# Gate/up pairs with three 2x2 blocks, and a hidden turn by way of DRAM

## The reference

```
def _swiglu(x, w_gate, w_up, w_down):
    return (jax.nn.silu(x @ w_gate) * (x @ w_up)) @ w_down
x = _layer_norm(DEEPNORM_ALPHA * x + _swiglu(x, w_gate, w_up, w_down), ln2_g, ln2_b)
# x (256, 2048), w_gate and w_up (2048, 5632), w_down (5632, 2048)
```

## Time and profile before

| | |
|---|---|
| median of three runs | 931.42 us (930.88 to 931.42) |
| the profiled execution, its own time | 931.67 us |
| its span, first to last instruction | 929.9 us |
| TensorE busy | 923.4 us, 99% |
| VectorE busy | 773.7 us, 83% |
| ScalarE busy | 513.4 us, 55% |
| GpSimd busy | 95.9 us, 10% |
| moved by DMA | 188.06 MB, mean 202 GB/s |

### The profile page before, as it was taken

One profiled execution on the slowest core, in us unless ns is written; L12 is line 12 of the kernel. 1 busy time (PEld: TensorE's weight loads), 2 busy tenths in 40 slices (PEclk: granted clock), 3 DMA queues, 4 the chain that ended last, 5 costly groups with the idle time before them and its releaser, 6 DMA issues.

```text
span 929.9 us, 11643 instructions
## 1 busy us (share of the span) xinstructions
PE 923.4 (99%) x4406; PEld 774.5 (83%) x4406; DVE 773.7 (83%) x1049; ACT 513.4 (55%) x704; POOL 95.9 (10%) x84
## 2 busy tenths in 40 slices
PE   9999999999999999999999999999999999999997
PEld 8999988888878888888888888888888888888885
DVE  6778566578779898989999998988969997999777
ACT  5686765354464646555565646455545565456550
POOL 0205530000311020202011020000000000000000
PEclk9999999999999999999999999999999999999999
DMA  9744324584808375665648375756657656355632
GB/s 362 315 166 145 129 91 167 195 328 167 318 5 290 111 256 162 223 218 185 228 135 274 112 270 148 242 198 200 219 210 300 226 225 233 130 222 231 230 132 91
DMA packets 36759, 188.06 MB, mean 202 GB/s; under 512 B 4064, under 2 KB 4576, under 8 KB 22880
## 3 DMA queue, kind: packets, MB, share of 16 engines
q1 hardware_dynamic: 36672, 187.32, 56.4%
q0 software_dynamic: 32, 0.00, 0.0%
HBM read 183.11 MB, written 4.19 MB: 201 GB/s over the span
## 4 chain that ended last, share of the span: by engine, by line
PE 99%; DVE 0%; ACT 0%; DVEq 0%; issue 0%; ACTq 0%
PE acc L1983 26%; PE acc L2005 21%; PE acc L1758 9%; PE tp L1983 9%; PE acc L1966 6%; PE acc L1696 5%; PE tp L1966 4%; PE tp L2005 4%; PE acc L1617 4%; PE acc L1895 2%; PE tp L1935 2%; PE acc L1730 1%; PE tp L1809 1%; PE tp L1744 1%; PE tp L1822 1%; PE tp L1606 0%
## 5 line engine op out<-in xcount | busy, mean ns | idle before, releaser
L1983 PE MATMUL acc<-w_hi,act_t 128*128 128x512 f32 x720 | 227.3, 389 | 0.0
L972 ACT ACTIVATE w_hi<-raw 128x1024 fp32r<-128x1024 f32 x120 | 125.7, 1057 | 111.4 <-PE acc L1983 57.2
L1021 ACT ACTIVATE w_hi<-raw 128x512 fp32r<-128x512 f32 (+1 forms) x154 | 114.9, 782 | 100.3 <-PE acc L2005 88.0
L2005 PE MATMUL acc<-w_hi,hid_t 128*128 128x512 f32 x504 | 161.0, 389 | 0.0
L1424 DVE TENSOR_TENSOR w_lo<-raw,w_hi 128x512 fp32r<-128x512 f32 (+1 forms) x154 | 131.8, 881 | 33.2 <-ACT w_hi L1021 33.0
L1983 PEld LDWEIGHTS acc<-w_hi,act_t 128*128 128x128 f32 x720 | 135.1, 188 | 28.1
L1377 DVE TENSOR_TENSOR w_lo<-raw,w_hi 128x1024 fp32r<-128x1024 f32 x120 | 147.2, 1244 | 7.7 <-ACT w_hi L972 6.9
L1983 PE MATMUL acc<-w_lo,act_t 128*128 128x512 f32 x360 | 140.0, 389 | 0.0
L2005 PEld LDWEIGHTS acc<-w_hi,hid_t 128*128 128x128 f32 x504 | 94.6, 188 | 19.6
L2005 PE MATMUL acc<-w_lo,hid_t 128*128 128x512 f32 x252 | 98.0, 389 | 0.0
L1374 DVE TENSOR_TENSOR w_lo<-raw,w_hi 128x1024 fp32r<-128x1024 f32 x63 | 82.7, 1313 | 18.2 <-ACT w_hi L967 17.8
(11 more groups left out here) (262 smaller groups left out, 1582.2 us busy)
## 6 DMA issues: line engine op xcount, KB each, us to landing
raw<-in_w_pairs SPq DMA_DIRECT2D x120, 512.0 KB, 4.5
raw<-in_w_down SPq DMA_DIRECT2D x44, 1024.0 KB, 6.0
raw<-in_w_pairs SPq DMA_DIRECT2D x18, 1024.0 KB, 7.6
raw<-in_w_out SPq DMA_DIRECT2D x16, 1024.0 KB, 4.9
raw<-in_w_gu SPq DMA_DIRECT2D x8, 1024.0 KB, 10.7
raw<-in_x_w SPq DMA_DIRECT2D x14, 552.0 KB, 7.1
raw<-in_w_uq SPq DMA_DIRECT2D x4, 1024.0 KB, 6.1
raw<-in_w_ukv SPq DMA_DIRECT2D x4, 1024.0 KB, 4.8
```

The lines of the kernel that those rows point to most:

```text
L972: act.activation(w_hi[:, v % RING, :], plain_raw(m), ACT.Copy).then_inc(hi_done, 1)
L1021: act.activation(unit_parts(u)[0], block_of(b, block, width), ACT.Copy).then_inc(down_hi_done, 1)
L1983: last = pe.matmul(out[:, t, :], act_t[:, k0 + m, x, t * P:(t + 1) * P], part[:, v % RING, m * GC:(m + 1) * GC], start=False, stop=(end an ...
L2005: last = pe.matmul(bank, lhs(x), part[:, cols * GC:(cols + 1) * GC], start=(first == u and (cols, x) == (0, 0) and part is hi_), stop=(end ...
```

## The change

Three blocks instead of two: `PAIR_K` becomes 6 and `PLAIN` 5. A product step is cut in two, "two" for the first two quads (1024 columns, 6 matmuls) and "third" for the third one (512 columns, 3 matmuls). The four ends of the second tile of the pair before (second 1 to 4) stand between the products P1, P5, P6, P7. The ring places are handed out in blocks of 512 columns by a new `ring_places`, for the gate/up and the down stage together: `BEFORE[v]` is the step that held the place, `FREED[v]` the first step that waits for v. Seeds, Silu and `gate_up` stand where `FREED` says. The sums T are cut in two as well. T3 moves behind second 1, T2 and T4 directly behind their product's half.

SP loads three quads: the first two behind plain load 4 (they wait for P4's split of the pair running), the third behind plain load 5.

The hidden values are turned by two transpositions over all 128 partitions into `local`, which turns each 32x32 block within its own 32 partitions. GpSimd then stores `local` to a DRAM buffer (512 KB) and loads it back with four DMAs of 32 partitions each (128 KB), which brings the blocks to their partitions. `turn_hid(p - 1)` stands behind first 1, `hid_hi` and `hid_lo` of a pair a whole pair after it. In the down stage the last pair is turned behind unit 5, and `hid_hi` of it still stands behind unit 13. `y_s` and `local` share memory, and so do the second half of `hid` and the sums `g_sum` of A.

```diff
 PAIRS = TILES // 2
-PAIR_K = 4
+BLOCKS = 3
+PAIR_K = 2 * BLOCKS
 PLAIN = (KD - PAIR_K) // 2
...
     for p in range(1, PAIRS):
-        ends = [(p - 1, "second", n) for n in range(PLAIN - 3, PLAIN)] if p > 1 else [None] * 3
-        for product, end in zip((P1, P5, P6), ends):
-            steps += [(p, "product", product), end]
-        steps += [(p, "product", n) for n in (P7, P2, P3)] + [(p, "first", 0), (p, "product", P4)]
-        steps += [(p, "first", n) for n in range(1, PLAIN)] + [(p, "second", n) for n in range(PLAIN - 3)]
-    steps += [(PAIRS - 1, "second", n) for n in range(PLAIN - 3, PLAIN)]
-    return tuple(step for step in steps if step)
+        for product, end in zip((P1, P5, P6, P7), range(1, PLAIN)):
+            steps += [(p, "two", product), (p, "third", product), (p - 1, "second", end)]
+        steps += [(p, part, product) for product in (P2, P3) for part in ("two", "third")]
+        steps += [(p, "first", 0), (p, "two", P4), (p, "third", P4)]
+        steps += [(p, "first", n) for n in range(1, PLAIN)] + [(p, "second", 0)]
+    steps += [(PAIRS - 1, "second", n) for n in range(1, PLAIN)]
+    return tuple(steps)
...
+HID_AT = 1
+LAST_HID_AT = 4
+BLOCK_MOVES = 4 * 16
...
-LAST_TURN = 11
+LAST_TURN = 5
+LAST_HID = 13
...
+    widths = [1 if kind == "third" else 2 for _, kind, _ in FFN_STEPS]
+    widths += [unit[3] for unit in DOWN_UNITS[:len(DOWN_UNITS) - LAST_LATE]]
+    at, places, before = 0, {}, {}
+    held = {x: V_PAIRS - RING + x // 2 for x in range(RING_BLOCKS)}
+    for v, width in enumerate(widths, V_PAIRS):
+        if at + width > RING_BLOCKS:
+            at = 0
+        places[v], before[v] = at, max(held[x] for x in range(at, at + width))
+        held.update((x, v) for x in range(at, at + width))
+        at = (at + width) % RING_BLOCKS
     return places, before
...
+FREED = {v: min(w for w in BEFORE if BEFORE[w] >= v) for v in range(V_PAIRS, V_DOWN)}
...
+                    if n == PLAIN_SLOTS and p < PAIRS - 1:
+                        load_quad(p + 1, 0)
+                        load_quad(p + 1, 1)
+                    if n == PLAIN_SLOTS + 1:
                         if p < PAIRS - 1:
-                            load_quad(p + 1, n - PLAIN)
-                        else:
-                            load_down(n - PLAIN)
+                            load_quad(p + 1, 2)
...
             def hid_hi(p):
-                act.wait_ge(ffn_turned, p + 1)
+                act.wait_ge(ffn_turned, BLOCK_MOVES * (p + 1))
                 if p < len(DOWN_QUADS):
                     act.wait_ge(s_step, 4 * p + 2)
-                act.activation(hid_of(p, 0), turned[:], ACT.Copy).then_inc(ffn_hi, 1)
+                act.activation(hid_blocks(p, 0), turned_blocks, ACT.Copy).then_inc(ffn_hi, 1)
...
-                if (kind, n) == ("second", PLAIN - 4):
-                    hid_hi(p - 1)
-                if (kind, n) == ("product", P5) and 2 <= p < len(DOWN_QUADS) + 2:
+                if (kind, n) == ("first", HID_AT) and p > 1:
+                    hid_hi(p - 2)
+                if (p, kind, n) == (PAIRS - 1, "second", LAST_HID_AT):
+                    hid_hi(PAIRS - 2)
+                if (kind, n) == ("third", P5) and 2 <= p < len(DOWN_QUADS) + 2:
                     q = p - 2
                     act.wait_ge(s_step, 4 * q + 4)
-                    act.activation(s_t[:, q, 0, :, :], s_sum[:], ACT.Copy).then_inc(s_hi, 1)
+                    act.activation(s_t[:, q, 0, :, :], s_sum[:, q, 1, :, :], ACT.Copy).then_inc(s_hi, 1)
...
+            def turn_hid(p):
+
+                dve.wait_ge(ffn_hid, 2 * p + 2)
+                if p > 0:
+                    dve.wait_ge(blocks_stored, 16 * p)
+                dve.wait_ge(y_added, 2 * min(p + 1, PAIRS - 1))
+                for i in range(2):
+                    dst = local[:, :, i, :, :, :].rearrange("p b c t s -> p t c b s")
+                    src = hid[:, i, :, :].rearrange("p t (c b s) -> p t c b s", c=2, b=4)
+                    last = dve.transpose(dst, src)
+                last.then_inc(local_done, 1)
...
-                if (kind, n) == ("product", P1):
-                    pair_sum(p, B11, B11, B12)
-                    pair_sum(p, B12, B12, B22)
-                if (kind, n) == ("product", P5):
-                    pair_sum(p, B11, B11, B22)
-                if (kind, n) == ("product", P2):
-                    pair_sum(p, B21, B11, B21)
-                if (kind, n) == ("first", 2):
+                if (kind, n) == ("third", P1):
+                    sum_1(p, "two")
+                    sum_1(p, "third")
+                if (kind, n) == ("second", 1) and p < PAIRS - 1:
+                    sum_3(p + 1, "two")
+                    sum_3(p + 1, "third")
+                if n == P5 and kind in ("two", "third"):
+                    sum_2(p, kind)
+                if n == P2 and kind in ("two", "third"):
+                    sum_4(p, kind)
+                if (kind, n) == ("first", HID_AT):
                     add_y(p)
-                if kind == "first" and n >= 2:
-                    turn_hid(p - 1, n - 2)
+                    if p > 1:
+                        hid_lo(p - 2)
+                    turn_hid(p - 1)
...
+            def blocks_store(p):
+
+                pool.wait_ge(local_done, p + 1)
+                if p > 0:
+                    pool.wait_ge(ffn_turned, BLOCK_MOVES * p)
+                pool.dma_start(blocks_out, local[:].rearrange("p b c i t s -> p b (c i t s)")).then_inc(blocks_stored, 16)
+
+            def blocks_load(p):
+
+                pool.wait_ge(blocks_stored, 16 * (p + 1))
+                if p > 0:
+                    pool.wait_ge(ffn_lo, p)
+                    pool.wait_ge(s_step, 4 * min(p, len(DOWN_QUADS)))
+                src = blocks_out.rearrange("(n p) b e -> b p n e", n=4)
+                for b in range(4):
+                    dst = turned[32 * b:32 * b + 32, :, :, :, :, :].rearrange("p n c i t s -> p n (c i t s)")
+                    pool.dma_start(dst, src[b]).then_inc(ffn_turned, 16)
+
+            for p in range(1, PAIRS):
+                if 0 <= p - 2 < len(DOWN_QUADS):
+                    factor_low(p - 2)
+                blocks_store(p - 1)
+                blocks_load(p - 1)
+                if p - 1 < len(DOWN_QUADS):
+                    factor_sums(p - 1)
+            blocks_store(PAIRS - 1)
+            blocks_load(PAIRS - 1)
```

366 lines of the change are left out of this document (202 added, 164 removed).

## The result

| | before | after |
|---|---|---|
| median | 931.18 us (930.88 to 931.42) | 997.61 us (995.12 to 999.03) |
| ratio, 95% interval | | 1.0711 (1.0689 to 1.0733) |
| span of the profiled execution | 929.9 us | 995.5 us |
| length of a pair, six in the middle (before: two) | 42.16 us | 49.75 us |
| length of the two behind them | | 43.76 us |

The kernel became 66 us slower. The forecast was 934.1 us, with a range to 947.0, so time and range were wrong, and only the sign was right, by luck: it was forecast from the third quad (b), and the way over DRAM (c) decided.

What follows compares the result with a forecast made beforehand. TensorE, busy 923.4 of 929.9 us, was taken to bound the kernel. Matmuls and seed wait gave -7.4, the third quad +10.1: span 932.6, time 934.1 us; range for 8 in 10, 926.0 to 947.0.

Steps and rivals of the forecast that it cites:

- (b): Third quad lands late for P1 third: 1.3 us short in pairs 2 to 8, 0.5 in 9 and 10; +10.1 us.
- (c): From transpositions over store, loads and sums to the `s_t` copy: 13.2 to 17.1 us, likely 15.5, within the 16 allowed.
- Matmuls: TensorE has 3 matmuls less in each of ten pairs, -6.80 us in all.
- VectorE's total: VectorE's work in a pair sums to 35.5 of 41.48 us, so the total fits.
- the transposition: VectorE's transposition over 128 partitions, two a pair: bounds 0.69 and 0.87 us, taken as 0.8.
- (a): From the end of `first` 4 over Silu to `second` 2: 9.3 us in 9.35; 0 to 0.75 short beside GpSimd.
- a rival of 19: GpSimd's way too long: sums end 19 us after transpositions, 2.9 us in each of pairs 2 to 8, 945.3; chance 0.15.
- the rival's conditions: GpSimd's store over DRAM costs 128 rows of several pieces, or its issue waits for VectorE.
- The down stage: Last turned pair needed behind unit 13, 13 us later; store and loads take 8.4 to 11.3, so no cost.
- the seed wait: TensorE's 0.7 us wait behind P6 of pair 1; 0.6 of it taken as gone.
- the larger gate sums: Gate sums at the start grow by half: nothing, or up to 0.6 us.
- The prediction's own test: In the profile after, ScalarE's `s_t` copy waiting for GpSimd means (c) decides; its split of P1 third waiting means the forecast.

Runs made afterwards that it cites:

- e11: e8 with GpSimd's four sums begun only after VectorE's split of `second` 2, and the `s_t` copy behind `second` 4: 928.0 us.
- e1: The changed kernel with ScalarE's copy into `s_t` behind P2 of the two blocks instead of behind P5 of the third: 961.1 us.
- e8: e1 with half of each quad loaded before the burst, and the last pair's `hid_hi` and `hid_lo` behind unit 19: 939.5 us.
- e12: e11 with the quads loaded whole, in the changed kernel's order: 950.4 us.
- e4: The changed kernel with quad loads of 64 columns instead of 2048 from pair 3 on: 957.2 us.
- e9: e1 with quad loads of 64 columns from pair 3 on, and the last pair's `hid_hi` and `hid_lo` behind unit 19: 941.0 us.
- e10: e8 with the copy into `s_t` back behind P5 of the third block: 948.8 us.
- e7: e5 with the last pair's `hid_hi` and `hid_lo` behind unit 19 instead of 13: 955.0 us.
- e5: e1 with the plain half for `second` 0 issued ahead of the second quad instead of behind it: 959.8 us.

## Why the prediction was right or wrong

**Matmuls.** Right: 4376 instead of 4406, and 41.5 us a pair where nothing waits (e11).

**VectorE's total and the transposition.** VectorE was busy 214.7 us in the six middle pairs, 35.8 a pair against 35.5, but by luck: the sum leaves out what GpSimd's operations cost it. By the same sum the kernel before had 36.5, and it held 38.6 (231.8 us in the six pairs from 367.11); e1 held 36.7 and e8 37.7. In the pair of the changed kernel shown above, the last three of the four sums ran while VectorE waited (from 513.29 to 516.74). Two transpositions over 128 partitions take 1.30 us together, 0.69 for one: the lower bound, where I took 0.8.

**(a) Ring and Silu.** Right that it just fits, right that GpSimd breaks it, wrong in which operation does: I named the one into `s_t`, and it was the four sums, 0.95 us against my 0 to 0.75. It was hidden behind (b) and (c) until those were gone.

**(b) The third quad.** The mechanism was right and the size too small. In e1, whose burst is that of the changed kernel, ScalarE starts on the third quad as it lands, at 435.01, 16.3 us after the split of `first` 0 ended (418.70), where I had 12.4 to 15.6 and took 15.0. By my own sum that is 2.6 us short and not 1.3, and e1 lost 2.9 a pair. The burst by itself cost 1.8 to 2.1 a pair in e12's fastest run, and 22.4 us in the median, where the forecast had 10.1 in all. I also missed the plain half that SP issues between the quads, which is needed first: ScalarE waited 4.8 us for it in the rows of after and 6.7 in those of e1.

**(c) The way over DRAM.** This is the step that failed. I gave 13.2 to 17.1 us, and a rival of 19; it was 22.1. The terms: store 9.9 against 4.0 to 5.3; loads 7.9 against 4.4 to 6.0; sums 4.0 against 4.8 to 5.8. I had seen that the store meets the burst, and allowed it 1.3 us more, its share of the bytes; it took 3.5 without the burst and 9.9 with it. Whether it stands behind the weights in a queue or shares their rate isn't told apart by these runs. For the loads I used landings of 2.2 to 3.8, one at a time; four of 128 KB landed in 6.1 us in the median with the burst, in 6.3 and 6.7 without it (e4, e9), and in 4.6 to 5.0 with half of each quad fetched early (e8, e10, e11), which isn't explained. The other side of the comparison, 16 us allowed, held: the way less what TensorE lost at `second` 2 is 17.6 - 1.7 = 15.9 in e4, 18.8 - 2.6 = 16.2 in e10 and 22.1 - 4.5 = 17.6 in the changed kernel.

By the Trainium skill, "DMA: Bandwidth & Descriptors", Anatomy of one DMA, the store is 3.2 us and a load 2.3 (both estimates from the page's figures). The trace agrees for the store without the burst (3.2 median in e4) and not for the loads (6.3 there). The rule prices one DMA alone, and I had said that by it (c) is no danger; 8.7 us in the changed kernel decides against that.

**The rival's price.** I priced it at the wait alone, 2.9 us for a way of 19. The seven pauses were 32.8 us, and the 12 matmuls behind each took 4.2 to 5.3 us instead of 2.72, 14.3 more in all by the clock: 47.1. Undoing them in e1 gave 36.5, since other waits, the burst's among them, then showed: in the six middle pairs, all else above 41.48 a pair rose from 10.1 to 18.6 us. Neither of the rival's conditions held: GpSimd issued the store in 0.58 us, and without the burst it landed in 3.2.

**The down stage.** Wrong: I gave the last pair 13 to 15 us and 8.4 to 11.3 of need, so nothing. From the store's issue at 761.54 to the end of ScalarE's wait at 780.75 it took 19.2 us, and cost 4.8 (e7). It is the same mis-sizing as (c).

**Pair 1.** I took 0.6 off for the seed wait and gave the larger gate sums "nothing, or up to 0.6". In e11 TensorE loses 3.4 us there (the waits of 1.6 and 0.8 above, one of 0.6 ahead of them, and their starts), beside GpSimd's low halves of the gate factors. No run moved these, so the cause is read from the rows alone. VectorE and GpSimd of e11, pair 1:

```profile
258.91 4.03 DVE L1456 TENSOR_TENSOR quad<-quad 128x1024 f32<-128x1024 f32 x2
...
258.90 3.48 POOL L1691 TENSOR_TENSOR s_gate<-g_sum,s_gate 128x1024 fp32r<-128x1024 f32 x1 [4.48 <-ACT s_third L999]
```

Two operations of 1.22 took 4.03. With it, 924.0 and 3.4 come near e11's 928.0.

**The sum of it.** From 997.6 down: the copy's place 36.5 (e1), the down stage 4.8 (e7 against e5), the burst 16.8 (e8 against e1, less that 4.8), the sums' and the copy's new place 11.5 (e11), which leaves 928.0. The order of loads, 1.3 in e5, isn't in e8 and e11. The terms hang on the order in which they are undone: put back into e11, the burst costs 22.4. The forecast kept only the burst's, with 10.1. The prediction's own test named the case rightly: if ScalarE's `s_t` copy waits for GpSimd, (c) decides.

## What to carry to other kernels

A store sent over DRAM can cost what is in flight beside it more than its own bytes (512 KB landed in 3.2 to 8.7 us here): sum up the weights that are under way when it is issued, price both directions with rows of the same size, and put the reader of it behind the longest of these, since an engine that waits in order holds all its later work. When a wait of TensorE's of several us is found, add what its clock takes back behind it. And three limits stood on one step here: each fix showed the next only when the one ahead was gone, so a change is to be judged by the runs that undo its limits one after another.
